# Attention slots with fixed PSUM bank roles, flip copies on two engines, and logarithms in the hybrid mask

## The chip, the cores and the metric

The kernel runs on one core of one Trainium2 chip. The metric is the device time of one execution in microseconds (us), lower is better. Engines are called by the profile's names: PE (TensorE, the matrix engine), DVE (VectorE), ACT (ScalarE), POOL (GpSimd) and SP (SyncE, which here only issues DMAs).

## The reference

A sequence of 256 positions and width 1024 passes through four layers in float32. Layer one (kind `a`): sliding-window attention with sinks, 16 heads, 2 key/value heads. Layer two (`b`): block attention, which for 256 positions is plain causal attention, 16 heads, 4 key/value heads. Layers three and four (`h`, the hybrids): 8 heads of attention beside a state space scan, and then a gated feed-forward part. Each attention is softmax(scores + mask) times values. In the hybrids three dilated windows are merged by their denominators:

```python
def dilated_attention(q, k, v):
    outs, lses = [], []
    for window, dilation in DILATED_PATTERNS:
        o, l = dilated_window_branch(q, k, v, window, dilation)
        outs.append(o)
        lses.append(l)
    wts = jax.nn.softmax(jnp.stack(lses, axis=0), axis=0)
    return jnp.einsum('ibshg,ibshgc->bshgc', wts, jnp.stack(outs, axis=0))
```

This equals one softmax in which each key counts as often as there are windows that hold it (0 to 3 times): a multiplicity per pair of positions.

## The kernel before, in words

The kernel is raw code for five engines, whose order is one list of steps, `sc.steps`, written out by `build_schedule` through `mixer_ab` (layers one and two) and `hybrid` (three and four). Every engine walks the same list and does its part of each step, so a step that stands earlier in the list is earlier on every engine; engines wait for each other by semaphores.

The bulk is projections. A step `chunk` is 12 matmuls for the first 128 positions, and the step `rest` behind it 12 for the second 128; a weight block of 512 columns takes two chunks (`halves`, one per half of the contraction). Weights are split into a high and a low part for precision: SP loads `raw` (L956), ACT rounds to `hi` (L1161), DVE or POOL forms `lo` (L901), two chunks ahead (`due`, `AHEAD`), and PE multiplies (L1000). The split of a chunk's step stands on each engine before the work put between `chunk` and `rest`.

Between `chunk` and `rest`, and between chunks, the lists of `halves`, `project_chunk` and `out_product` place other work (`goes_on`). One such piece is `attention(sc, n)`, slot n of a layer. It works on pairs of heads:

- `scores`: PE computes scores of two heads (L1052, L1055, 64-row tiles), each in its own bank of 128x384 f32 (three 128x128 blocks: the causal half of 256x256). DVE adds the mask and takes row minima of the negated scaled scores in place (L1644), ACT takes exponentials into `prob` (L1293, L1294).
- `flip`: PE transposes the three blocks of `prob` into a bank (L975). In layers one and two ACT copies the bank to `probT` (L1301); in the hybrids DVE does so and multiplies by the multiplicities `mult` (L1654).
- `pv`: PE multiplies `probT` by the values with a column of ones (L1075 to L1077), both heads into one bank, and ACT copies it out as `oev` (L1308).

Slot n of the kernel before does, in this order: outputs (`pv`, `oev`) of pair n-2, flips of pair n-1, scores of pair n. Layers one and two have slots 0 to 9, the hybrids 0 to 5.

PSUM has eight banks. Four (0 to 3) hold projections. The other four ("scratch banks", `NSCR`) are handed out by `Schedule.bank` in rotation to all small steps: flips, scores, outputs, and helpers such as `turn_q` and `turn_k` (transposes of queries and keys, copied by ACT at L1283 and L1277), `turn` (transposes of gated outputs or inputs: ACT copies at L1211, DVE subtracts at L1580, and only then is the bank free), `conv` (transposes at L975, ACT scales at L1333, DVE adds the other taps in six instructions at L1736 and frees the bank), `sums`, `decay` and others. PE waits in `freed` (L869) until the engine that last used the bank is done with it. A full slot takes five banks of four: the second bank of the scores is the one that the same slot's outputs used.

Where the slots stand: in `mixer_ab` slots 1, 2, 3 around the chunks of the first gate projection, with two `turn_q` steps ahead of slot 3; slot 4 right behind the two silus `ev_z` (L1244, with an ACT table load); slots 5 to 7 around the second gate projection, with `fill_gates` (on POOL, L1431 and L1436) behind slot 5; two `turn` steps ahead of slot 8; slot 9 inside the first chunk of the output product, and `fill_gates` of the second half behind that chunk's `rest`. In `hybrid`: slot 1 then `sums`; `conv` for block 0; slot 2 then `conv`; `conv_silu` (four silus on ACT, L1340, with a table load) then slot 3; `conv`; slot 4 then `conv`; `conv_silu` then slot 5 and `fill_gates`.

At the start ACT issues small loads (L1169 to L1177): sinks, positions, small rows, the masks (`mask_stage`, L1174), then the convolution taps (`taps_stage`, L1175 and L1177), which PE transposes once (L1020) ahead of the third projection.

Of the kernel before, what the change touches and what calls it, by code (L numbers as in the profile page):

```python
# [24 lines left out]
BF16 = mybir.dt.bfloat16  # L25
# [9 lines left out]
NEG = -1e30  # L35
# [26 lines left out]
C_SEL = C_MASK + 3 * QC + P  # L62
C_ALL = C_SEL + 32
M_SCAN, M_SEL = 3 * QC, 3 * QC + P


def constants():
# [7 lines left out]
    mult = [(d >= 0) * ((d <= 128).astype(np.float32) + (d % 4 == 0) + (d % 16 == 0)) for d in delta]  # L75
    for i, x in enumerate(mult):
        c[:, C_CT + i * P:C_CT + (i + 1) * P] = x.T
    inv = np.float32(10000.0) ** (-np.arange(0, HD, 2, dtype=np.float32) / np.float32(HD))
    for m in range(M):
# [8 lines left out]
        [x > 0 for x in mult],  # L88
# [5 lines left out]
    c[:, C_MASK + 3 * QC:C_SEL] = np.where(t > u, NEG, 0.0)  # L94
# [42 lines left out]
class Schedule:  # L137


    def __init__(self):  # L140
        self.steps, self.count, self.blocks, self.banks = [], {}, [], []
# [3 lines left out]
        self.heads, self.loaded, self.mult_flips, self.plain_flips = 0, 0, 0, 0  # L145
# [7 lines left out]
    def bank(self):  # L153
        n = len(self.banks)
        b = Bank(n % NSCR, self.banks[n - NSCR] if n >= NSCR else None)
        assert b.before is None or b.before.freed is not None, "a bank is taken before it is freed"
        self.banks.append(b)
        return b
# [56 lines left out]
def attention(sc, n):  # L215
# [182 lines left out]
def new_attention(sc, which, heads, nkv):  # L398
    if sc.heads:
        count_flips(sc)  # L400
# [4 lines left out]


def count_flips(sc):
    if sc.att["kind"] == "h":
        sc.mult_flips += len(sc.att["flip"])
    else:  # L410
        sc.plain_flips += len(sc.att["flip"])


def mixer_ab(sc, which, w_in, w_out, nkv, mid=False):
# [36 lines left out]
    if mid:  # L451
# [7 lines left out]
        0: (att(9), [lambda: fill_gates(sc, a, 1, zb)]),  # L459
# [3 lines left out]
def hybrid(sc, layer, w, last_gain):  # L463
# [108 lines left out]
    b = halves(sc, w_in, [(z0, 512)], do(conv_silu, 1) + att(5) + do(fill_gates, sc, a, 0, None), do(conv, 2, 0) + do(bback),  # L572
# [120 lines left out]
def build(nc, t):  # L693
# [37 lines left out]
    masks = keep("masks", [P, 3 * QC + P + 32], BF16)  # L731
# [21 lines left out]
    mult = cst[:, C_CT:C_CT + QC]  # L753
# [219 lines left out]
    def _(pe):  # L973
# [4 lines left out]
        for s in sc.steps:  # L978
# [87 lines left out]
            elif s.kind == "pv":  # L1066
# [3 lines left out]
                pe.wait_ge(sem["flip", "vector" if a["kind"] == "h" else "scalar"], a["flip"][hd].n + 1)  # L1070
# [80 lines left out]
    def _(act):  # L1151
# [37 lines left out]
        for s in sc.steps:  # L1189
# [106 lines left out]
            elif s.kind == "flip" and s.att["kind"] != "h":  # L1296
# [4 lines left out]
                done(nc.scalar.activation(A[f"probT{s.p % 2}"][:, :], psum[4 + s.bank.at][:, 0:QC], ACT.Copy), s)  # L1301
# [155 lines left out]
    def _(dve):  # L1457
# [81 lines left out]
        for s in sc.steps:  # L1539
# [99 lines left out]
            elif s.kind == "scores":  # L1639
                a, hd = s.att, s.head  # L1640
                dve.wait_ge(sem["scores", "tensor"], s.i + 1)
                bank, at_ = psum[4 + s.bank.at], {"a": 0, "b": 1, "h": 2}[a["kind"]] * QC
                for m, c in enumerate((slice(0, P), slice(P, QC))):
                    last = nc.vector.tensor_tensor_reduce(  # L1644
                        bank[:, c], bank[:, c], masks[:, at_ + c.start:at_ + c.stop], -SCALE,
# [3 lines left out]
            elif s.kind == "flip" and s.att["kind"] == "h":  # L1649
# [4 lines left out]
                done(tt(Hb[f"probT{s.p % 2}"][:, :], psum[4 + s.bank.at][:, 0:QC], mult, ALU.mult), s)  # L1654
# [160 lines left out]
```

## Time and profile before

| what | us |
|---|---|
| median of 3 runs | 920.56 |
| lowest and highest of the runs | 919.92, 925.25 |
| the profiled execution | 923.07 |
| its span (first to last instruction) | 921.2 |
| PE busy in the span | 882.9 |
| DVE, ACT, POOL busy | 558.5, 518.6, 127.7 |

The profiled execution's own time is its span and 1.9 us around it; it lies 2.5 us above the median. PE's busy time counts a matmul from its start to its modelled end, so neighbours overlap, and a row's length is a little more than the distance to the next start.

### The profile page before, as it was taken

Reading aid. Unit: us, or ns where it says so; the run is one execution under the profiler, and the core shown is the slowest. Engines: PE = TensorE matmul, PEld = TensorE weight load, DVE = VectorE, ACT = ScalarE, POOL = GpSimd, SP = SyncE. Lnnn points to the kernel's source line nnn. Section 1 sums busy time; section 2 is a strip of 40 time slices with the busy share of each in tenths; the row PEclk is TensorE's granted clock in tenths of the full one; section 3 lists DMA queues with packets and bytes.
Section 4 is the critical chain, followed back from the end, with each engine's and each line's share of the span. In section 5 each row is a group of like instructions: output and inputs, shape, how many; then the busy total and the mean of one; then the engine's idle time right before and its main releaser. Section 6 shows DMA issues by size and latency. Waiting matters only on the chain.

```text
span 921.2 us, 12293 instructions
## 1 busy us (share of the span) xinstructions
PE 882.9 (96%) x4557; PEld 728.8 (79%) x4557; DVE 558.5 (61%) x969; ACT 518.6 (56%) x853; POOL 127.7 (14%) x103
## 2 busy tenths in 40 slices
PE   4899998999999999999999999999999999999995
PEld 3787887878787888788888888887888888888884
DVE  4754578546766567865555544756677755555443
ACT  3567755676487685464444433677874644444331
POOL 0031103421015350000000000042430000000000
PEclk9899999999999999999999999999999999999998
DMA  8641344443544424576565555534423766565521
GB/s 279 218 150 57 129 163 157 140 129 102 177 167 139 137 93 136 164 236 187 188 185 183 183 183 185 193 104 139 137 92 120 246 190 188 186 190 189 196 95 46
DMA packets 94846, 146.88 MB, mean 159 GB/s; under 512 B 6476, under 2 KB 54852, under 8 KB 94788
## 3 DMA queue, kind: packets, MB, share of 16 engines
q1 hardware_dynamic: 91392, 139.14, 46.3%
q0 software_dynamic: 1440, 5.24, 2.0%
q10 hardware_dynamic: 1956, 1.71, 0.5%
q8 instruction: 37, 0.61, 0.3%
q14 instruction: 21, 0.17, 0.1%
HBM read 145.04 MB, written 1.05 MB: 159 GB/s over the span
## 4 chain that ended last, share of the span: by engine, by line
PE 70%; issue 21%; DVE 3%; ACT 2%; DMA 2%; POOL 0%; ACTq 0%; POOLq 0%; DVEq 0%
PE bank L1000 55%; PE bank L975 6%; PE bank L1141 1%; PE bank L1052 1%; PE bank L1055 1%; PE bank L1077 1%; PE bank L1076 1%; DMA taps_stage<-in_conv_b 1%; PE bank L1075 1%; DMA gains<-in_norm_g 1%; ACT junk L1186 1%; DVE lo L901 1%; ACT hi L1161 1%; DVE hyb_MT L1749 1%; PE bank L1120 0%
## 5 line engine op out<-in xcount | busy, mean ns | idle before, releaser
L901 DVE TENSOR_TENSOR lo<-raw,hi 128x1024 fp32r<-128x1024 f32 x246 | 302.4, 1254 | 133.7 <-ACT hi L1161 131.6
L1161 ACT ACTIVATE hi<-raw 128x1024 fp32r<-128x1024 f32 x262 | 268.4, 1056 | 77.0 <-PE bank L1000 69.9
L1000 PE MATMUL bank<-hi,xT_hi 128*128 128x512 f32 (+2 forms) x736 | 294.4, 400 | 8.5 <-DVE lo L901 3.1
L1000 PE MATMUL bank<-hi,xT_lo 128*128 128x512 f32 (+2 forms) x736 | 285.5, 388 | 0.0
L1000 PE MATMUL bank<-lo,xT_hi 128*128 128x512 f32 (+2 forms) x736 | 284.5, 387 | 0.0
L1000 PEld LDWEIGHTS bank<-hi,xT_hi 128*128 128x128 f32 x736 | 140.0, 190 | 41.6 <-issue 13.8
L1000 PEld LDWEIGHTS bank<-hi,xT_lo 128*128 128x128 f32 x736 | 139.6, 190 | 28.9
L1000 PEld LDWEIGHTS bank<-lo,xT_hi 128*128 128x128 f32 x736 | 140.3, 191 | 25.5 <-issue 0.5
L1000 PE MATMUL bank<-hi,hT 128*128 128x512 f32 x352 | 111.2, 395 | 0.0
L1000 PEld LDWEIGHTS bank<-hi,hT 128*128 128x128 f32 x352 | 66.3, 188 | 15.4
L1000 PE MATMUL bank<-lo,hT 128*128 128x512 f32 x176 | 69.4, 395 | 0.0
L1000 PE MATMUL bank<-hi,oT_hi 128*128 128x512 f32 x160 | 66.9, 418 | 0.0
L1000 PE MATMUL bank<-hi,oT_lo 128*128 128x512 f32 x160 | 62.7, 392 | 0.0
L1000 PE MATMUL bank<-lo,oT_hi 128*128 128x512 f32 x160 | 62.4, 390 | 0.0
L1208 ACT ACTIVATE hT<-bank 128x512 fp32r<-128x512 f32 x22 | 13.2, 598 | 77.2 <-PE bank L975 77.2
L1577 DVE TENSOR_TENSOR hT<-bank,hT 128x512 fp32r<-128x512 f32 x22 | 15.2, 692 | 59.3 <-ACT hT L1208 59.3
L975 PE MATMUL bank<-cst,quarter 128*128 128x128 f32 x264 | 39.4, 277 | 12.0 <-DVE quarter L1571 10.1
L1258 ACT ACTIVATE silu_gate<-bank,rms 128x256 f32<-128x256 f32 x44 | 20.7, 475 | 50.3 <-PE bank L1000 50.3
L975 PEld LDWEIGHTS bank<-cst,quarter 128*128 128x128 f32 x264 | 32.8, 143 | 20.2 <-issue 10.3
L901 POOL TENSOR_TENSOR lo<-raw,hi 128x1024 fp32r<-128x1024 f32 x16 | 38.2, 2399 | 74.1 <-ACT hi L1161 74.1
L1612 DVE SCALAR_TENSOR_TENSOR quarter<-bank,rms,silu_gate 128x256 f32<-128x256 f32 x44 | 19.3, 479 | 41.1 <-ACT silu_gate L1258 41.1
L1736 DVE SCALAR_TENSOR_TENSOR hyb_acc<-bank,taps,hyb_acc 128x255 f32<-128x255 f32 (+2 forms) x72 | 29.2, 474 | 19.9 <-ACT hyb_acc L1333 19.9
(230 smaller groups left out, 983.5 us busy)
## 6 DMA issues: line engine op xcount, KB each, us to landing
raw<-in_w_in SPq DMA_DIRECT2D x26, 1024.0 KB, 5.1
raw<-in_w_gate SPq DMA_DIRECT2D x44, 512.0 KB, 4.0
raw<-in_w_up SPq DMA_DIRECT2D x44, 512.0 KB, 4.9
raw<-in_w_down SPq DMA_DIRECT2D x22, 1024.0 KB, 4.9
raw<-in_w_out SPq DMA_DIRECT2D x20, 1024.0 KB, 5.1
raw<-in_w_in_b SPq DMA_DIRECT2D x10, 1024.0 KB, 5.1
raw<-in_w_in_a SPq DMA_DIRECT2D x8, 1024.0 KB, 7.8
gains<-in_norm_g POOLq DMA_DIRECT2D x2, 512.0 KB, 6.8
```

Source lines behind the costliest of these rows:

```text
L901: return engine.tensor_tensor(lo[r][:, cols], raw[c.i % RAW][:, cols], hi[r][:, cols].bitcast(F32), ALU.subtract)
L975: return nc.tensor.transpose(out, in_, ident)
L1000: last = nc.tensor.matmul(bank[:, 0:wd], still[a], mv[r][:, off:off + wd], start=c.first and i == 0 and j == 0, stop=c.last and i == len(t ...
L1052: nc.tensor.matmul(bank[:, 0:P], q[r:r + 64, hd // 2, 0:P], k[r:r + 64, kv, 0:P], start=True, stop=True)
L1055: nc.tensor.matmul(bank[:, P:QC], q[r:r + 64, hd // 2, P:S], k[r:r + 64, kv, 0:S], start=True, stop=True).then_inc(sem["scores", "tensor"], 1)
L1075: nc.tensor.matmul(bank[:, c0:c0 + W1], pt[:, 0:P], v[:, 0, kv, :], start=True, stop=True)
L1161: nc.scalar.activation(hi[c.i % SPLIT][:, cols], raw[c.i % RAW][:, cols], ACT.Copy)\
L1208: done(nc.scalar.activation(out, bank[:, :], ACT.Copy), s)
L1258: last = nc.scalar.activation(sil[s.i % 2][:, m, :], bank[:, 0:UPW], ACT.Silu, scale=rms[:, 1, m:m + 1])
L1577: done(tt(b, bank[:, :], a.bitcast(F32), ALU.subtract), s)
L1612: last = stt(quarter[s.buf][:, m * UPW:(m + 1) * UPW], psum[2 * s.block["pair"] + m][:, UPW:2 * UPW], rms[:, 1, m:m + 1], sil[s.i % 2][:, ...
L1736: ins = stt(acc[:, tap:S], x[:, 0:S - tap], cw[:, 3 - tap, ct:ct + 1], acc[:, tap:S], ALU.mult, ALU.add)
```

## The change

1. In `attention`, slot n does flips of pair n-1, scores of pair n, outputs of pair n-1. The last slot (9, or 5 in the hybrids) disappears from the lists, and `fill_gates` of the second half in `mixer_ab` moves from behind the `rest` of the output product's first chunk to between that `chunk` and its `rest`.
2. Banks have roles: scores of the even and odd head in banks 0 and 1, their flips in 2 and 3, outputs in bank 2. Other steps take the bank least recently taken, where scores count as taken three places later than they were.
3. The flip copy of the even head is on ACT, of the odd head on DVE, in all layers, as plain copies.
4. The hybrids' multiplicities m are added as log(m)/SCALE with the mask before the exponential, in f32 from `cst`, in place of the bf16 mask and the later multiplication. The mask tensor loses 384 of its 1312 columns.

```diff
-C_SEL = C_MASK + 3 * QC + P
+C_SEL = C_MASK + 2 * QC + P
@@ constants
-        c[:, C_CT + i * P:C_CT + (i + 1) * P] = x.T
+        c[:, C_CT + i * P:C_CT + (i + 1) * P] = np.where(x > 0, np.log(np.maximum(x, 1)) / SCALE, NEG)
@@ Schedule
-    def bank(self):
-        n = len(self.banks)
-        b = Bank(n % NSCR, self.banks[n - NSCR] if n >= NSCR else None)
+    def bank(self, at=None, later=0):
+        if at is None:
+            at = min(range(NSCR), key=lambda i: self.taken[i])
+        b = Bank(at, self.banks[at])
         assert b.before is None or b.before.freed is not None, "a bank is taken before it is freed"
-        self.banks.append(b)
+        self.banks[at] = b
+        self.clock += 1
+        self.taken[at] = self.clock + later
         return b
@@ attention
-    if 2 <= n <= pairs + 1:
-        a["obank"] = sc.bank()
-        for head in (2 * n - 4, 2 * n - 3):
-            s = sc.step("pv", head=head, att=a, bank=a["obank"], p=a["base"] + head)
-            a["pv"].append(s)
-        o = sc.step("oev", att=a, pair=head // 2, bank=a["obank"], pv=s)
-        a["obank"].freed = (o, "scalar")
-        a["oev"].append(o)
     if 1 <= n <= pairs:
         for head in (2 * n - 2, 2 * n - 1):
-            b = sc.bank()
-            s = sc.step("flip", head=head, att=a, bank=b, p=a["base"] + head,
-                        n=len(a["flip"]) + (sc.mult_flips if a["kind"] == "h" else sc.plain_flips))
-            b.freed = (s, "vector" if a["kind"] == "h" else "scalar")
+            b = sc.bank(2 + head % 2)
+            s = sc.step("flip", head=head, att=a, bank=b, p=a["base"] + head, n=(a["base"] + head) // 2)
+            b.freed = (s, "vector" if head % 2 else "scalar")
             a["flip"].append(s)
     if n < pairs:
-        b0, b1 = sc.bank(), sc.bank()
+        b0, b1 = sc.bank(0, 3), sc.bank(1, 3)
...
+    if 1 <= n <= pairs:
+        a["obank"] = sc.bank(2)
+        for head in (2 * n - 2, 2 * n - 1):
+            s = sc.step("pv", head=head, att=a, bank=a["obank"], p=a["base"] + head)
+            a["pv"].append(s)
+        o = sc.step("oev", att=a, pair=head // 2, bank=a["obank"], pv=s)
+        a["obank"].freed = (o, "scalar")
+        a["oev"].append(o)
@@ mixer_ab, out_product
-        0: (att(9), [lambda: fill_gates(sc, a, 1, zb)]),
+        0: ([lambda: fill_gates(sc, a, 1, zb)], ()),
@@ hybrid
-    b = halves(sc, w_in, [(z0, 512)], do(conv_silu, 1) + att(5) + do(fill_gates, sc, a, 0, None), do(conv, 2, 0) + do(bback),
+    b = halves(sc, w_in, [(z0, 512)], do(conv_silu, 1) + do(fill_gates, sc, a, 0, None), do(conv, 2, 0) + do(bback),
@@ ACT
-            elif s.kind == "flip" and s.att["kind"] != "h":
+            elif s.kind == "flip" and s.head % 2 == 0:
...
-                done(nc.scalar.activation(A[f"probT{s.p % 2}"][:, :], psum[4 + s.bank.at][:, 0:QC], ACT.Copy), s)
+                done(nc.scalar.activation(B[f"probT{s.p % 2}"][:, :], psum[4 + s.bank.at][:, 0:QC], ACT.Copy), s)
@@ DVE
+                mask = {"a": masks[:, 0:QC], "b": masks[:, QC:2 * QC], "h": log_mult}[a["kind"]]
...
-            elif s.kind == "flip" and s.att["kind"] == "h":
+            elif s.kind == "flip" and s.head % 2:
...
-                done(tt(Hb[f"probT{s.p % 2}"][:, :], psum[4 + s.bank.at][:, 0:QC], mult, ALU.mult), s)
+                done(nc.vector.tensor_copy(B[f"probT{s.p % 2}"][:, :], psum[4 + s.bank.at][:, 0:QC]), s)
```

## Rows read from the trace of the kernel before

**Rows 1.** The page, busy us, share of the span and instructions of PE first.
```profile
PE 882.9 (96%) x4557; PEld 728.8 (79%) x4557; DVE 558.5 (61%) x969; ACT 518.6 (56%) x853; POOL 127.7 (14%) x103
```

**Rows 2.** Waits of PE, whole span: total us, times, longest us.
```profile
PE bank L1020 <- DMA taps_stage<-in_conv_b: 3.1, 1, 3.1
...
PE bank L1052 <- ACT hyb_o L1308: 2.7, 2, 1.4
...
PE bank L1052 <- ACT attn_o L1308: 2.5, 2, 1.3
...
PE bank L975 <- DVE quarter L1683: 0.3, 1, 0.3
```

**Rows 3.** Timeline (start us, length us), PE and ACT, layer one slot 2.
```profile
62.00 0.33 PE L1075 MATMUL bank<-attn_v,attn_probT 128*128 128x65 f32 x2
...
63.28 0.82 PE L975 MATMUL bank<-cst,attn_prob 128*128 128x128 f32 x6
...
64.03 0.49 PE L1052 MATMUL bank<-attn_kT,attn_qT 64*128 64x128 f32 x4
...
64.89 0.50 PE L1000 MATMUL bank<-hi,xT_hi 128*128 128x512 f32 x1
...
67.15 1.06 ACT L1161 ACTIVATE hi<-raw 128x1024 fp32r<-128x1024 f32 x1
```

**Rows 4.** Timeline, PE and DVE, layer one slot 1.
```profile
57.49 0.81 PE L975 MATMUL bank<-cst,attn_prob 128*128 128x128 f32 x6
...
57.98 1.85 DVE L901 TENSOR_TENSOR lo<-raw,hi 128x1024 fp32r<-128x1024 f32 x1 [1.75 <-ACT hi L1161]
```

**Rows 5.** Lines L1301 and L1654: duration ns min/median/max.
```profile
L1301 ACT ACTIVATE attn_probT<-bank x32: 484/491/511, 58.0 to 215.5; 128x384 f32<-128x384 f32 x32
...
L1654 DVE TENSOR_TENSOR hyb_probT<-bank,cst x16: 547/550/558, 276.7 to 642.0; 128x384 f32<-128x384 f32 x16
```

**Rows 6.** Timeline, PE and ACT, query turns ahead of layer one slot 3.
```profile
67.75 1.03 PE L975 MATMUL bank<-cst,attn_q 128*128 128x128 f32 x8
...
68.39 1.08 ACT L1283 ACTIVATE attn_qT<-bank 128x512 f32<-128x512 f32 x2 [0.18 <-PE bank L975]
```

**Rows 7.** Timeline, ACT and PE, layer one slot 4.
```profile
74.85 1.28 ACT L1244 ACT_TABLE_LOAD   x1
...
76.15 1.26 ACT L1244 ACTIVATE attn_z<-bank,rms 128x512 f32<-128x512 f32 x2
...
77.84 0.49 PE L1052 MATMUL bank<-attn_kT,attn_qT 64*128 64x128 f32 x4 [1.30 <-ACT attn_o L1308]
```

**Rows 8.** Timeline, ACT and DVE, gate turns ahead of layer one slot 8.
```profile
99.49 1.09 ACT L1211 ACTIVATE oT_hi<-bank 128x512 fp32r<-128x512 f32 x2 [0.18 <-PE bank L975]
...
100.48 1.28 DVE L1580 TENSOR_TENSOR oT_lo<-bank,oT_hi 128x512 fp32r<-128x512 f32 x2
```

**Rows 9.** Timeline, layer three, slots 1, 2 and 4.
```profile
276.21 0.82 PE L975 MATMUL bank<-cst,hyb_prob 128*128 128x128 f32 x6
...
277.25 1.07 ACT L1161 ACTIVATE hi<-raw 128x1024 fp32r<-128x1024 f32 x1
...
284.05 2.43 DVE L1736 SCALAR_TENSOR_TENSOR hyb_acc<-bank,taps,hyb_acc 128x255 f32<-128x255 f32 x6 [2.07 <-ACT hyb_acc L1333]
...
284.51 0.33 PE L1075 MATMUL bank<-hyb_v,hyb_probT 128*128 128x65 f32 x2
...
286.73 0.49 PE L1052 MATMUL bank<-hyb_kT,hyb_qT 64*128 64x128 f32 x4
...
304.60 1.22 DVE L901 TENSOR_TENSOR lo<-raw,hi 128x1024 fp32r<-128x1024 f32 x1
```

**Rows 10.** DMA landings; windows of PE, PEld, DVE, ACT, POOL busy, PEclk, DMA, GB/s.
```profile
mask_stage<-in_cst ACTq DMA_DIRECT2D x1, 656.0 KB, 9.2
...
38.00:40.00 2.00, 1.45 (x4) 1.26 (x5) 1.97 (x3) 0.27 (x1) 0.00 (x0) 0.50 0.94 351
...
50.00:110.00 60.00, 58.70 (x370) 48.33 (x370) 30.70 (x85) 44.19 (x85) 14.70 (x13) 1.00 0.30 100
```

More of the change, by code:

```diff
@@ L61 @@
 C_MASK = C_KEEP
-C_SEL = C_MASK + 3 * QC + P
+C_SEL = C_MASK + 2 * QC + P
 C_ALL = C_SEL + 32
-M_SCAN, M_SEL = 3 * QC, 3 * QC + P
+M_SCAN, M_SEL = 2 * QC, 2 * QC + P
 def constants():
@@ L74, in constants @@
     c[:, C_U:C_U + P] = t <= u
-    mult = [(d >= 0) * ((d <= 128).astype(np.float32) + (d % 4 == 0) + (d % 16 == 0)) for d in delta]
+    mult = [(d >= 0) * ((d <= 128).astype(np.float64) + (d % 4 == 0) + (d % 16 == 0)) for d in delta]
     for i, x in enumerate(mult):
-        c[:, C_CT + i * P:C_CT + (i + 1) * P] = x.T
+        c[:, C_CT + i * P:C_CT + (i + 1) * P] = np.where(x > 0, np.log(np.maximum(x, 1)) / SCALE, NEG)
     inv = np.float32(10000.0) ** (-np.arange(0, HD, 2, dtype=np.float32) / np.float32(HD))
@@ L87, in constants @@
         [d >= 0 for d in delta],
-        [x > 0 for x in mult],
     )
@@ L93, in constants @@
             c[:, at:at + P] = np.where(x, 0.0, NEG)
-    c[:, C_MASK + 3 * QC:C_SEL] = np.where(t > u, NEG, 0.0)
+    c[:, C_MASK + 2 * QC:C_SEL] = np.where(t > u, NEG, 0.0)
     for part in range(3):
@@ L140, in __init__ @@
     def __init__(self):
-        self.steps, self.count, self.blocks, self.banks = [], {}, [], []
+        self.steps, self.count, self.blocks = [], {}, []
+        self.banks, self.taken, self.clock = [None] * NSCR, [0] * NSCR, 0
         self.parts, self.quarters, self.gains = 0, [], []
@@ L144, in __init__ @@
         self.pool_splits = []
-        self.heads, self.loaded, self.mult_flips, self.plain_flips = 0, 0, 0, 0
+        self.heads, self.loaded = 0, 0
     def step(self, kind, **of):
@@ L398, in new_attention @@
 def new_attention(sc, which, heads, nkv):
-    if sc.heads:
-        count_flips(sc)
     a = sc.att = {"kind": which, "heads": heads, "nkv": nkv, "scores": [], "flip": [], "pv": [], "oev": [],
@@ L404, in new_attention @@
     return a
[L407 to L411, printed above, removed]
 def mixer_ab(sc, which, w_in, w_out, nkv, mid=False):
@@ L730, in build @@
     cst = keep("cst", [P, C_KEEP])
-    masks = keep("masks", [P, 3 * QC + P + 32], BF16)
+    masks = keep("masks", [P, 2 * QC + P + 32], BF16)
     csum = keep("csum", [P, P], BF16)
@@ L752, in build @@
     ident, upper = cst[:, C_ID:C_ID + P], cst[:, C_U:C_U + P]
-    mult = cst[:, C_CT:C_CT + QC]
+    log_mult = cst[:, C_CT:C_CT + QC]
     base = place[0]
@@ L1069, in _ @@
                 kv = hd // (a["heads"] // a["nkv"])
-                pe.wait_ge(sem["flip", "vector" if a["kind"] == "h" else "scalar"], a["flip"][hd].n + 1)
+                pe.wait_ge(sem["flip", "vector" if hd % 2 else "scalar"], a["flip"][hd].n + 1)
                 bank = freed(pe, s.bank) if hd % 2 == 0 else psum[4 + s.bank.at]
@@ L1295, in _ @@
                                           bias=shift[:, hd, 1:2]), s)
-            elif s.kind == "flip" and s.att["kind"] != "h":
+            elif s.kind == "flip" and s.head % 2 == 0:
+                B = Hb if s.att["kind"] == "h" else A
                 act.wait_ge(sem["flip", "tensor"], s.i + 1)
@@ L1641, in _ @@
                 dve.wait_ge(sem["scores", "tensor"], s.i + 1)
-                bank, at_ = psum[4 + s.bank.at], {"a": 0, "b": 1, "h": 2}[a["kind"]] * QC
+                bank = psum[4 + s.bank.at]
+                mask = {"a": masks[:, 0:QC], "b": masks[:, QC:2 * QC], "h": log_mult}[a["kind"]]
                 for m, c in enumerate((slice(0, P), slice(P, QC))):
                     last = nc.vector.tensor_tensor_reduce(
-                        bank[:, c], bank[:, c], masks[:, at_ + c.start:at_ + c.stop], -SCALE,
+                        bank[:, c], bank[:, c], mask[:, c], -SCALE,
                         sinks[:, 1, hd:hd + 1] if a["kind"] == "a" else BIG, ALU.add, ALU.min,
@@ L1648, in _ @@
                 done(last, s)
-            elif s.kind == "flip" and s.att["kind"] == "h":
+            elif s.kind == "flip" and s.head % 2:
+                B = Hb if s.att["kind"] == "h" else A
                 dve.wait_ge(sem["flip", "tensor"], s.i + 1)
```

## The prediction, made before the changed kernel was built or run

> **What bounds the kernel now.** I read the page's first part, then TensorE's waits, then the timeline of single attention slots on TensorE, ScalarE (ACT) and VectorE (DVE). TensorE is busy for 882.9 of 921.2 us [rows 1], so only two things can change the time: work that TensorE itself does, and gaps in its stream. The change keeps every TensorE instruction (six transposes, four scores matmuls and six output matmuls a pair of heads), so only gaps count. TensorE's waits name few of them [rows 2]: four slots wait for the copy of the outputs (2.7 + 2.5 = 5.2 us), one gate quarter costs 0.3, the taps 3.1. The rest lies at the start and in the norms, which the change leaves alone.
>
> A whole slot runs from 62.00 (outputs) over 63.28 (flips) and 64.03 (scores) to 64.89, the next weight matmul [rows 3]: 2.89 us, of which outputs 1.28, flips 0.65 to 0.75, scores the rest. Then come 12 weight matmuls (2.87, to 67.75 in rows 6) and the next slot. ACT has finished the exponentials 2.26 us after the scores' end and only then splits weights (67.15) [rows 3]; DVE's split follows, 1.22 us when alone [rows 9]. A producer's end reaches the waiting engine after about 0.2 us from TensorE and 0.15 from ACT or DVE: four of the eight transposes from 67.75 are through at 68.19 (0.109 each, as 0.65 for six), and ACT starts at 68.39 [rows 6].
>
> **The change part by part.** Four edits move TensorE's gaps.
>
> *1. Scores get banks of their own.* Now the second scores bank is the outputs' bank of the same slot, so scores wait for ACT's output copy. The 1.30 us at 77.84 [rows 7], its three siblings, a hidden 0.2 in slot 2 of layer three (scores at 286.73, 2.22 after 284.51 [rows 9], where rows 3 have 2.03) and the gate's 0.3 go: -5.7.
>
> *2. Outputs move into the slot of their flips.* Order in a slot: flips, scores, outputs. From slot start T: flips end T+0.65, scores T+1.55, first outputs may start T+1.55, second T+2.17. The even head's copy on ACT costs 0.49 [rows 5] and is ready at 0.33+0.2+0.49+0.15 = T+1.2. The odd head's on DVE isn't in the trace: from above the 0.55 of the multiply that it replaces, from below half of that, since it reads one operand for two [rows 5]; I take 0.5, near the multiply, which reads the same bank into the same tile. At 0.28 the terms below lose 0.2 each in six places, 1.3 in all. It is ready at T+1.55. So a slot with both engines idle gets no wait. The exceptions, each an engine busy at T:
> - Slot 1 of the first two layers: DVE, slowed beside GpSimd's rotation, splits until 57.98+1.85 = 59.83 against T = 57.49 [rows 4]; copy and signal end at 60.4, wanted at 59.66: 0.75 each, 1.5 together.
> - Slot 1 of layer three: ACT's split ends at 278.32, where T = 276.21 [rows 9]; copy to 278.9, wanted 277.76: 1.15. In layer four ACT is free: 0.
> - Slot 4 (layers one and two) and slot 3 (three and four): ACT loads a table and does the silus, 1.28 + 1.26 [rows 7] (four silus in the hybrids). Exponentials now end 1.3 earlier against the next slot, but the output copy (0.4) comes before the split; the load starts at T-0.4 and the even copy is ready at T+2.8, wanted T+1.55: 1.25, 1.25, 1.3, 1.3 = 5.1. The old wait is thus replaced, not removed.
> - Slot 6 of layers one and two, where GpSimd's gates stretch DVE's split to about 1.9: 0.25 each, 0.5.
> - Slot 8 of layers one and two has no scores between flips and outputs: the even copy is wanted at T+0.65, ready T+1.12: 0.47 each, 0.9.
> - Slot 4 of the hybrids: DVE's split of 304.60, 1.22 long [rows 9], stands ahead of the odd copy; outputs come 0.7 late, twice: 1.4.
>
> *3. Flips are tied to banks 2 and 3, and other work takes the banks least recently taken.* I followed the taking of banks. Scores' banks are marked three places younger, so a helper before a slot gets 3 and then 2, and the slot's first flip needs 2 at once. Before, the outputs' 1.28 us and the rotation covered that.
> - Query turns before slot 3 of layers one and two: eight transposes from 67.75 end at 68.62 (0.87); ACT's copies end at 68.39+1.08 = 69.47 [rows 6]; with the signal 69.62: 1.0 each, 2.0.
> - Gate turns before slot 8: ACT starts at 99.49, so by the spacing of rows 6 the transposes ran from 98.85 to 99.72; ACT's pair ends at 100.58 and DVE's second subtraction (1.28 for two) about 0.7 later [rows 8]; with the signal 1.73 late each, 3.5. I let DVE's own split no longer be what it queues behind; if it still is, 2.2 each.
> - The first convolution before slot 2 of the hybrids: its bank is 2, and DVE's six taps end at 284.05+2.43 = 286.48 while the slot starts at 284.51 [rows 9], 2.1 late. The sums ahead of it move back with the slot and lose a queue of 0.4: 1.7. The same chain in layer four, whose rows repeat these, ends 1.1 late instead of 2.0: 1.0 after the change. Together 2.7.
> - The second convolution before slot 4 holds bank 3: the odd flip waits 0.57, twice: 1.1.
>
> *4. Masks shrink by 384 columns.* Their load is 656 KB and lands 9.2 us after issue [rows 10]; the taps, issued behind it, are what TensorE waits 3.1 for [rows 2]. 192 KB less is 0.56 us at the 351 GB/s of that time [rows 10], and 2.7 at the mask's own pace (656 KB in 9.2 us), of which much is waiting to start; I take 0.9. More would be worth more: behind this gap the granted clock is 0.50 [rows 10], the lower of the two levels (1.2 of 2.4 GHz), about 2.6 us for 13 matmuls. I expect that it stays. The DVE cast of masks gets shorter behind other work, and f32 logarithms in place of a bf16 mask lie in a pass beside weight matmuls: 0, between -0.1 and +0.5 over the 16 heads.
>
> **Sum.** New waits: 1.5 + 1.15 + 5.1 + 0.5 + 0.9 + 1.4 (edit 2, 10.6) and 2.0 + 3.5 + 2.7 + 1.1 (edit 3, 9.3) = 19.9. Gone: 5.7 and 0.9. Net +13.3. Against the profiled execution (923.07 us, span 921.2) that is 936.4; against the median of 920.56, 933.9. The dropped last slot of each layer saves nothing, since its outputs are done one slot earlier.
>
> Two rules of the Trainium skill speak here. The trace has the table load at 1.28 and the silu right behind it, at 76.15 after 74.85 [rows 7]. "ScalarE: Activation LUTs", What ACT_TABLE_LOAD costs, adds a drain of about 1.38 us to each switch; four slots would then lose 5.5 more. The trace shows no such drain, so I leave it out.
>
> **The rivals.**
> - *The copies hide (12%).* If helpers have left bank 2 and both copies fit under the scores everywhere, only the removals stay: 920.56 - 6.6 = 914.0. For it: ordinary slots have 0.6 us of room (wanted T+2.17, ready T+1.55). Against it: rows 6, 8 and 9 show the holders still working after T. It decides if the waits before flips and outputs sum to less than 6.6 us.
> - *Only banks and tables bind (22%).* DVE's and ACT's splits drift earlier, as exponentials now end earlier, and the remaining copy waits (5.5) vanish: 933.9 - 5.5 = 928.4.
> - *The clock falls as well (16%).* After the 3.1 us gap the granted clock was 0.50; the 1.30 us gap at 77.84 [rows 7] left it at 1.00 over 50 to 110 us [rows 10]. The new 1.7 + 0.5 in slot 8 lies between. A fall costs some 2.6 us of matmuls; in both slots, 939.1. "TensorE: Matmul & The Clock Gate", A second HAM failure mode, says that small idles from cycling PSUM banks can make the clock oscillate; if that held in all eight stalled slots, the time would be near 955, which the clock of 1.00 around the present stalls of 1.2 to 1.4 us doesn't bear out.
>
> The forecast has 50%, 929 to 939 of its own.
>
> **How the numbers follow.** About 1% is what a measurement of this kernel tells from no change: 911.4 and 929.8 are the bounds. Slower: 0.44 of the forecast, 0.05 of the second rival, 0.15 of the third: 0.64. Faster by over 1% would need the first rival and the taps gap with its slow clock gone as well: 0.04. The rest, 0.32, is within. Range 922 to 941: it cuts off the first rival and the far end of the third.
>
> **What would show it.** Right: TensorE waits for ACT at the query flips (1.0) and for DVE at the gate flips (1.7) and at the flips after the first convolution (1.0 to 1.7); output matmuls wait for DVE's copy in slot 1 and behind table loads by 1.2 to 1.3; scores never wait for the outputs; the taps gap is 2 to 2.6. Wrong: no TensorE wait on flips, or named new waits under 10 us in sum; a taps gap under 1 us with the clock at 1.00 behind it; or a granted clock under 0.9 inside the attention stretches.

## The result and the profile after

The changed kernel takes 937.62 us (median of four runs, 931.89 to 938.57) where the kernel before takes 920.79 beside it (919.92 to 925.25): a ratio of 1.0157, 95% interval 1.0112 to 1.0202. It is slower. A second comparison of the same kernel, told below, gives 1.0137 (1.0112 to 1.0161) and a median of 931.81.

The profiled execution after took 931.89 us with a span of 930.0; the one before had 923.07 and 921.2. First the page's first part, for [rows 1]:

```profile
span 930.0 us, 12293 instructions
...
PE 883.9 (95%) x4557; PEld 727.6 (78%) x4557; DVE 559.3 (60%) x977; ACT 515.4 (55%) x845; POOL 125.5 (13%) x103
```

PE has the same 4557 matmuls and is busy for 1.0 us more than in [rows 1], so what came is almost all gaps. On balance eight copies moved from ACT to DVE (845 against 853, 977 against 969): sixteen of the first two layers went to DVE and eight of the hybrids to ACT. The waits of PE over the whole span (total us, times, longest), for [rows 2]:

```profile
PE bank L968 <- DVE oT_lo L1574: 3.3, 2, 1.7
...
PE bank L1068 <- ACT hyb_probT L1295: 2.9, 3, 1.0
...
PE bank L1013 <- DMA taps_stage<-in_conv_b: 2.7, 1, 2.7
...
PE bank L968 <- DVE hyb_acc L1732: 2.4, 4, 0.8
PE bank L1068 <- ACT attn_probT L1295: 2.2, 4, 0.8
PE bank L968 <- ACT attn_qT L1276: 1.7, 2, 0.8
...
PE bank L1068 <- DVE hyb_probT L1650: 0.7, 2, 0.4
PE bank L1068 <- DVE attn_probT L1650: 0.7, 2, 0.4
```

The four waits for output copies (5.2 us in [rows 2]) are gone, and no scores matmul waits at all. In their place stand three rows of waits of flips for their bank (L968: oT_lo, hyb_acc, attn_qT, 7.4 us together) and four rows of waits of output matmuls for a flip copy (L1068, 6.5 us): 13.9 us of named waits. (Lines have moved: transposes L975 to L968, scores L1052 to L1045, outputs L1075 to L1068, ACT's flip copy L1301 to L1295, DVE's L1654 to L1650.)

Single slots show each kind. The timeline (start, length, engine and line, what it waited for) of layer one, slots 1, 3, 4 and 8:

```profile
56.76 1.84 DVE L894 TENSOR_TENSOR lo<-raw,hi 128x1024 fp32r<-128x1024 f32 x1 [1.75 <-ACT hi L1154]
...
58.52 0.55 DVE L1650 COPY attn_probT<-bank 128x384 f32<-128x384 f32 x1
...
59.12 0.44 PE L1068 MATMUL bank<-attn_v,attn_probT 128*128 128x65 f32 x2 [0.37 <-DVE attn_probT L1650]
...
69.11 1.08 ACT L1276 ACTIVATE attn_qT<-bank 128x512 f32<-128x512 f32 x2 [1.25 <-PE bank L968]
70.34 0.84 PE L968 MATMUL bank<-cst,attn_prob 128*128 128x128 f32 x6 [0.83 <-ACT attn_qT L1276]
...
75.58 1.28 ACT L1237 ACT_TABLE_LOAD   x1
...
76.19 0.81 PE L968 MATMUL bank<-cst,attn_prob 128*128 128x128 f32 x6
76.88 1.26 ACT L1237 ACTIVATE attn_z<-bank,rms 128x512 f32<-128x512 f32 x2
...
78.03 0.49 ACT L1295 ACTIVATE attn_probT<-bank 128x384 f32<-128x384 f32 x1
...
78.67 0.41 PE L1068 MATMUL bank<-attn_v,attn_probT 128*128 128x65 f32 x2 [0.81 <-ACT attn_probT L1295]
...
101.53 1.29 DVE L1574 TENSOR_TENSOR oT_lo<-bank,oT_hi 128x512 fp32r<-128x512 f32 x2 [0.61 <-ACT oT_hi L1204]
102.96 0.85 PE L968 MATMUL bank<-cst,attn_prob 128*128 128x128 f32 x6 [1.66 <-DVE oT_lo L1574]
...
104.15 0.41 PE L1068 MATMUL bank<-attn_v,attn_probT 128*128 128x65 f32 x2 [0.34 <-ACT attn_probT L1295]
```

Read each as a chain. Slot 1: the split of 56.76 ends at 58.60, DVE's copy follows it and ends at 59.07, and the odd head's outputs start then. Slot 3: ACT's copy of the query turns ends at 70.19 and the flips start 0.15 later. Slot 4: the flips are there at 76.9, but ACT is in the table load and the silus until 78.1, and the even head's outputs wait 0.81. Slot 8: DVE's second subtraction ends at 102.82, and only then is bank 2 free for the first flip. Layer three: outputs of slot 1, flips of slot 2 behind the first convolution, and slot 4 with both waits:

```profile
283.78 0.41 PE L1068 MATMUL bank<-hyb_v,hyb_probT 128*128 128x65 f32 x2 [0.95 <-ACT hyb_probT L1295]
...
290.14 2.43 DVE L1732 SCALAR_TENSOR_TENSOR hyb_acc<-bank,taps,hyb_acc 128x255 f32<-128x255 f32 x6 [2.15 <-ACT hyb_acc L1327]
...
292.72 0.85 PE L968 MATMUL bank<-cst,hyb_prob 128*128 128x128 f32 x6 [0.80 <-DVE hyb_acc L1732]
...
312.59 0.52 PE L968 MATMUL bank<-cst,hyb_prob 128*128 128x128 f32 x3 [0.41 <-DVE hyb_acc L1732]
...
314.10 0.44 PE L1068 MATMUL bank<-hyb_v,hyb_probT 128*128 128x65 f32 x2 [0.37 <-DVE hyb_probT L1650]
```

A wait row counts from the modelled end of the last matmul, and in a running stream the next matmul starts before that end: the eight gate turns start at 100.27 and are through 8 x 0.109 later, at 101.14, where their row ends at 101.30. So a stop costs some 0.2 us more than its row says, and the slots must be measured as well. The measure used from here on is the slot distance: from the start of the last weight matmul before a slot to the start of the first one behind it. Over all slots and the gate quarters it grows by 18.3 us where it grows. It falls by 5.6 where the old waits were, and by 0.6 because the last slots are gone: +12.1 (the table further down has the parts).

Executions of the changed kernel scatter more than those of the kernel before (standard deviation 3.2 us over 14 against 1.5 over 45), and they differ with TensorE's mean granted clock: over the 14, 929.31, 930.33 and 930.37 at a mean of 0.998; 931.16 to 932.38 at 0.996; 935.08 to 935.34 at 0.989 to 0.991; 936.88 to 938.57 at 0.986 to 0.989. A straight line through all 14 has 0.66 us for each 0.001 of the mean. The kernel before has 0.991 to 0.997; the line through its 41 executions with a recorded clock has 0.81. At equal clock the two lines differ by about 13 us: 931.5 against 918.2 at 0.996, 934.8 against 922.2 at 0.991.

The two profiled executions differ by only 8.8 us of span. The slots account for +12.1 and the taps gap for -0.4 (2.7 for 3.1). The rest, about -3, is the clock: the execution before had 0.69 at 152 to 156 us and 0.68 and 0.50 at 36 to 44, the one after 1.00, and 0.78 and 0.79.

### The profile page after: what moved, and what is told of

It is laid out like the page before. It is cut to its first block, busy times and chain, and to the rows that moved or that the text cites. A ratio compares the mean times of both kernels' runs of the same rounds, so it can differ in the third digit from the quotient of the medians.

```text
span 930.0 us, 12293 instructions
## 1 busy us (share of the span) xinstructions
PE 883.9 (95%) x4557; PEld 727.6 (78%) x4557; DVE 559.3 (60%) x977; ACT 515.4 (55%) x845; POOL 125.5 (13%) x103
## 4 chain that ended last, share of the span: by engine, by line
PE 62%; issue 22%; DVE 8%; ACT 5%; DMA 2%; POOL 0%; ACTq 0%; POOLq 0%; DVEq 0%
PE bank L993 49%; PE bank L968 5%; DVE lo L894 2%; PE bank L1068 1%; PE bank L1134 1%; ACT hi L1154 1%; PE bank L1070 1%; PE bank L1069 1%; DMA taps_stage<-in_conv_b 1%; DVE hyb_acc L1732 1%; ACT junk L1179 1%; DMA gains<-in_norm_g 1%; PE bank L1048 1%; PE bank L1045 1%; DVE hyb_MT L1745 1%
## 5 line engine op out<-in xcount | busy, mean ns | idle before, releaser
L968 PE MATMUL bank<-cst,quarter 128*128 128x128 f32 x264 | 39.8, 279 | 11.9 <-DVE quarter L1565 10.2
L968 PEld LDWEIGHTS bank<-cst,quarter 128*128 128x128 f32 x264 | 33.0, 144 | 20.2 <-issue 10.4
```

The source lines that it names most:

```text
L968: return nc.tensor.transpose(out, in_, ident)
```

## The experiments

The theory to test was the prediction's: the change costs in two ways, flips that wait for a helper's bank, and outputs that wait for copies. Rivals: the order of the slots itself, the logarithms and the plain copy, or the clock. All kernels but two are the changed kernel, as it is or with a part undone; `log_only` and `outputs_dve` start from the kernel before. Each is compared with the others in two ways: by its time against the lines above at the same mean clock, and by the slot distances of its trace.

**1. The changed kernel again,** with no edit, timed beside the next three.

> The changed kernel itself, profiled and timed once more. Its profiled execution took 931.9 us at a mean clock of 0.996, its other executions 935 to 939 us at 0.986 to 0.991. Theory 1 (new waits of TensorE are the loss, the clock is a separate lottery that both kernels take part in): a median near 937 us against 921; where the clock is lower, it is low behind the long gaps that the kernel before has too (the taps near 38 us, the issue gap near 150 us), not in attention slots. Theory 2 (the new stalls pull the clock down): windows at half clock behind slot 8 of the first two layers or in the hybrids' slots.

Measured: 931.81 (929.31 to 936.88, six runs) against 920.64 (17 runs of the kernel before); ratio 1.0137 (1.0112 to 1.0161). The slowdown repeats. The median is lower because four of these six executions had a mean clock of 0.996 or more; the two at 0.986 and 0.989 took 936.88 and 935.34. The median near 937 that theory 1 expected was the lower clock's. Its waits of flips and outputs are those of the first profile.

**2. `lru_banks`: the roles of the banks undone.** Every piece takes the bank least recently taken; order, copies and logarithms stay.

```diff
-            b = sc.bank(2 + head % 2)
+            b = sc.bank()
...
-        b0, b1 = sc.bank(0, 3), sc.bank(1, 3)
+        b0, b1 = sc.bank(), sc.bank()
...
-        a["obank"] = sc.bank(2)
+        a["obank"] = sc.bank(a["flip"][2 * n - 2].bank.at)
```

> Only the bank roles undone: every step takes the least recently taken bank, the outputs take the bank of the even flip. Theory 1: flips no longer wait for query turns (1.7 us in the changed kernel's profile), gate turns (3.3) and convolutions (2.4), so 7.4 us less than the changed kernel, about 930 us, and at most 0.5 us of waits on other banks in their place. Rival (the order is what costs, the flips' waits only hide waits of the outputs for their copies): the output matmuls then wait 2 us or more longer in the same slots and the time stays above 934 us.

Measured: 926.72 (924.36 to 928.43, six runs); ratio 1.0062 (1.0044 to 1.008). PE's waits:

```profile
PE bank L1068 <- ACT hyb_probT L1295: 3.6, 5, 1.0
...
PE bank L1068 <- ACT attn_probT L1295: 2.5, 4, 0.8
...
PE bank L1045 <- ACT attn_qT L1276: 0.3, 2, 0.2
```

No flip waits for a helper. Copy waits stay and grow a little (7.6 for 6.5, with 0.8 and 0.7 on DVE's copies), since slots that start on time ask for their copies earlier. In slot 4 of the hybrids this takes back the whole gain, as the rival had it: the flip's wait of 0.41 is gone, the even output waits 0.34 in its place, and the slot distance stays at 3.72. In all the slot distances fall by 6.0, and against the changed kernel's line at the same clock (0.9938, 933.0) the run saves 6.6: half the slowdown is the bank roles. The expected 930 was reckoned from executions at a lower clock, so the 926.7 is not a larger gain than the 7.4 foretold but a smaller one.

**3. `later_zero`: the roles stay, the offset of three goes.** Helpers then take scores' banks as well as the flips'.

```diff
-        b0, b1 = sc.bank(0, 3), sc.bank(1, 3)
+        b0, b1 = sc.bank(0), sc.bank(1)
```

> Only the mark that makes the scores' banks three places younger is taken away; roles and order stay. A pair of helpers before a slot then gets banks 3 and 0 in place of 3 and 2. Theory 1 (the second helper sits in the even flip's bank): the flips' wait for query turns falls from 0.83 us each to under 0.2, that for gate turns from 1.66 to about 0.85 (the odd flip still waits for the first turn), the first convolutions' from 0.8 to about 0.5 (now a wait of the scores); 3.5 us less than the changed kernel at the same clock, 928 to 929 us. Rival (the wait is for the helper's copy whichever bank it sits in): no more than 1 us less.

Measured: 928.83 (928.45 to 929.26, four runs at 0.991 to 0.993), ratio 1.0096 (1.008 to 1.0112). Its waits on banks:

```profile
PE bank L968 <- DVE oT_lo L1574: 1.5, 2, 0.7
...
PE bank L968 <- DVE hyb_acc L1732: 0.8, 2, 0.4
...
PE bank L1045 <- DVE hyb_acc L1732: 0.4, 2, 0.3
```

The flips' waits fall from 7.4 to 2.3, and scores gain 0.4. The slot distances fall by 5.2 of the 6.0 that undoing the roles gives, and at the same clock the time falls by 5.6 of 6.6 (3.5 was expected): most of what the roles cost comes from the one argument that marks scores' banks as younger, so that helpers land on the banks that the next slot's flips need. In slot 8 the wait moves from the first flip (1.66) to the odd one (0.74), and the output wait behind it goes.

**4. `table_slots_dve`: in the four slots behind a table load, DVE copies both flips.** (Semaphores are counted by engine for that.)

```diff
-            s = sc.step("flip", head=head, att=a, bank=b, p=a["base"] + head, n=(a["base"] + head) // 2)
-            b.freed = (s, "vector" if head % 2 else "scalar")
+            who = "vector" if head % 2 or n == (3 if a["kind"] == "h" else 4) else "scalar"
+            s = sc.step("flip", head=head, att=a, bank=b, p=a["base"] + head, n=sc.flips[who], what=who)
...
+            b.freed = (s, who)
```

> The changed kernel with both flip copies on DVE in the four slots where ACT stands behind a table load and silus. Theory 1: the waits of output matmuls for ACT's copy in these slots (0.81, 0.69, 0.98, 0.97 us) shrink to 0.3 or less each, so 3 us less than the changed kernel, about 934.5 us. Rival (ACT's lateness only moves on, to the exponentials and the weight split behind them): the next slots get waits for ACT and the gain is under 1 us.

Measured: 931.03 (930.23 to 931.62, four runs, all at 0.990 to 0.992, where the changed kernel's line has about 935); ratio 1.0112 (1.0095 to 1.0129). Layer one, slot 4:

```profile
77.51 1.02 DVE L1653 COPY attn_probT<-bank 128x384 f32<-128x384 f32 x2
...
78.56 0.44 PE L1071 MATMUL bank<-attn_v,attn_probT 128*128 128x65 f32 x2
```

The outputs no longer wait, and the waits for ACT's copies fall from 2.9 + 2.2 to 0.9 + 0.7. The four slots shorten to 3.19 and 3.20, the distance of an ordinary slot, by 3.6 us together; at equal clock the time falls by 4.2. The table slots are worth 3.6 to 4.2 us, not 5.1. The next slots get no wait for ACT, so the rival is out.

**5. `lru_and_table_dve`: both of these,** to see what is left.

> The rotation of banks (run lru_banks) together with both flip copies on DVE in the four slots behind table loads (run table_slots_dve). Theory 1: the two gains add, -5.1 to -6.7 and -3.6 at the same clock, so 922.5 to 923.5 us, still 2 us above the kernel before, because slot 1's and slot 8's waits (some 2.4 us) stay and the old order has none of them. Rival (they overlap, one behind the other in the same slots): 925 us or more.

Measured: 922.09 (917.64 to 924.74, twelve runs), ratio 1.0021 (1.0006 to 1.0037). The two gains add, as theory 1 had it: the slot distances fall by 9.6, which is 6.0 and 3.6, and at equal clock the time falls by 10.4 where the two runs alone gave 6.6 and 4.2. Left over the kernel before are 2.5 of the 12.1 us by slot distances and 2.8 at equal clock. These are the copy waits of slots 1 and 8 and of the hybrids' slot 4, and the ordinary slots (below), less the old waits; no run removes them one by one.

**6. `old_order`: the slots' old order and rotation,** with the two-engine copies and the logarithms kept.

```diff
+    if 2 <= n <= pairs + 1:
+        a["obank"] = sc.bank()
+        for head in (2 * n - 4, 2 * n - 3):
...
-            b = sc.bank(2 + head % 2)
+            b = sc.bank()
...
-        b0, b1 = sc.bank(0, 3), sc.bank(1, 3)
+        b0, b1 = sc.bank(), sc.bank()
...
```

The outputs behind the scores go, and the last slots come back to the lists.

> The order of the slots and the rotation of the banks as before the change; the copies on two engines and the logarithms in the mask stay. Theory 1: the four waits of scores for the output copy are back (5.2 us), none of the 13.9 us of new waits is left, the taps gap is 2.7 in place of 3.1: 920.5 us, the same as before the change within 1.5 us. Rival (odd copies behind DVE's splits cost in this order too): 924 us or more, with output matmuls or flips waiting for DVE.

Measured: 922.64 (917.56 to 924.37, twelve runs), ratio 1.0017 (1.0003 to 1.0032), most of them at 0.991 or 0.992, where the kernel before has about 922: 0.7 us slower at equal clock. By medians it is 2.0 above, a little outside the expected 1.5. Its waits are those of [rows 2] again, and one more, in slot 1 of layer three, where the matmuls of `sums` wait for the bank that ACT's flip copy holds:

```profile
PE bank L1045 <- ACT hyb_o L1302: 2.7, 2, 1.4
...
PE bank L1045 <- ACT attn_o L1302: 2.5, 2, 1.3
...
PE bank L1076 <- ACT hyb_probT L1295: 0.9, 1, 0.9
```

That slot takes 3.46 us where the kernel before has 2.50, and slot 2 behind it 3.54 for 3.73; all other slot distances are those of the kernel before. So two engines for the copies cost 0.8 us, all of it in layer three, and no output matmul waits for DVE: the rival is out. The slowdown is the new order with its roles.

**7. `log_only`: logarithms alone in the kernel before,** with the smaller mask and DVE's plain copy.

```diff
-C_SEL = C_MASK + 3 * QC + P
+C_SEL = C_MASK + 2 * QC + P
...
-                done(tt(Hb[f"probT{s.p % 2}"][:, :], psum[4 + s.bank.at][:, 0:QC], mult, ALU.mult), s)
+                done(nc.vector.tensor_copy(Hb[f"probT{s.p % 2}"][:, :], psum[4 + s.bank.at][:, 0:QC]), s)
...
```

The table of logarithms and the mask argument change as in the change above.

> The kernel before with the logarithms in the mask alone: smaller mask load, f32 mask in the hybrids, a plain DVE copy in place of the multiplication, in the old order and rotation. Theory 1: worth nothing that can be measured, 920 to 921 us; the taps gap varies between 2.7 and 3.8 us from execution to execution, and a plain copy takes 0.56 us as the multiplication took 0.55. Rival (192 KB less ahead of the taps shorten the gap): the taps gap is under 2.5 us and the time 1 us or more below the kernel before.

Measured: 921.44 (917.24 to 923.66, twelve runs), ratio 1.0005 (0.9991 to 1.002). No difference can be told, and at equal clock it is 0.2 us. PE at the taps, and the mask's landing (KB, us from issue):

```profile
37.91 0.46 PE L1019 MATMUL bank<-cst,taps_stage 120*128 120x120 f32 x1 [2.59 <-DMA taps_stage<-in_conv_b]
...
mask_stage<-in_cst ACTq DMA_DIRECT2D x1, 464.0 KB, 8.4
```

The mask lands 0.8 earlier than in [rows 10]. The gap is 2.6 us here, but 3.1, 3.3 and 3.9 in `old_order`, `lru_banks` and `later_zero`, which have the same small mask, and 2.6 to 3.1 over five executions of the changed kernel: it varies by more from execution to execution than the edit moves it, and the time doesn't follow.

**8. `outputs_dve`: `log_only`, and DVE copies the outputs out in the four table slots.** This attacks the wait that the change was exposed to, without moving anything: ACT is busy behind its table load, and DVE takes the one copy.

```diff
-        o = sc.step("oev", att=a, pair=head // 2, bank=a["obank"], pv=s)
-        a["obank"].freed = (o, "scalar")
+        who = "vector" if n == (3 if a["kind"] == "h" else 4) else "scalar"
+        o = sc.step("oev", att=a, pair=head // 2, bank=a["obank"], pv=s, what=who, n=sc.oevs[who])
+        sc.oevs[who] += 1
+        a["obank"].freed = (o, who)
```

> The kernel before with the logarithms in the mask and one change more: in the four slots behind table loads DVE, not ACT, copies the outputs out, so that scores needn't wait behind ACT's silus. Theory 1: the four waits of scores (1.30, 1.18, 1.33, 1.37 us) shrink to 0.3 or less each, 4.5 us less than before: 916 us, faster than both kernels. Rival (another wait takes the place at once, for the exponentials or the weight split): 919 us or more.

Measured: 914.27 (911.53 to 916.25, six runs), ratio 0.9938 (0.992 to 0.9956): 5.7 us faster than the kernel before by medians (920.0, 23 runs) and 5.0 at equal clock, and faster than the changed one. Layer one, slot 4:

```profile
73.56 1.28 ACT L1253 ACT_TABLE_LOAD   x1
73.57 1.23 DVE L910 TENSOR_TENSOR lo<-raw,hi 128x1024 fp32r<-128x1024 f32 x1 [1.75 <-ACT hi L1170]
...
74.72 0.42 DVE L1663 COPY attn_o<-bank 128x260 f32<-128x260 f32 x1
...
75.29 0.49 PE L1061 MATMUL bank<-attn_kT,attn_qT 64*128 64x128 f32 x4
```

The copy (0.42 us) slips in between DVE's split and its next work, the scores start at 75.29 with no wait, PE's waits name no output copy any more, and the distance between the weight matmuls around the slot is 3.25 us for 4.50 before. The four slots together get 5.2 us shorter.

**9. `look_one`, `look_two`, `look_three`: three more profiled executions of the changed kernel,** for the clock.

> The changed kernel once more for its profile alone: where does the granted clock fall in a slower execution (935 us and more at a mean of 0.986 to 0.989)? Theory 1 (falls behind the taps gap and the issue gap only, which the kernel before has as well): low windows at 36 to 46 and 152 to 160 us alone, and a time on the line of about 0.6 us for each 0.001 of mean clock. Theory 2 (the new waits pull it down too, as at 104 to 108 us in the profile of table_slots_dve and at 280 to 288 us in that of later_zero): in some profile a low window inside an attention stretch.

> A second profile for the same question, with the same expectations: Theory 1 low windows at 36 to 46 and 152 to 160 us alone; theory 2 in some profile of the changed kernel a low window inside an attention stretch, costing some 2 us each.

> A third profile for the same question, with the same expectations as the two looks before: theory 1 low windows only behind the taps gap and the issue gap; theory 2 also one inside an attention stretch.

Measured: 935.08 (mean clock 0.989), 930.37 (0.998) and 931.16 (0.996), beside 918.8 for the kernel before. The first shows what the third rival foretold. Timeline of layer two's slot 8, and the windows of 4 us from it on (us, then PE, PEld, DVE, ACT, POOL busy with counts, granted clock, DMA share, GB/s):

```profile
218.85 0.85 PE L968 MATMUL bank<-cst,attn_prob 128*128 128x128 f32 x6 [1.66 <-DVE oT_lo L1574]
...
220.04 0.41 PE L1068 MATMUL bank<-attn_v,attn_probT 128*128 128x65 f32 x2 [0.34 <-ACT attn_probT L1295]
```
```profile
220.00:224.00 4.00, 3.96 (x16) 3.70 (x17) 0.29 (x1) 1.42 (x2) 0.00 (x0) 0.55 0.28 110
224.00:228.00 4.00, 4.00 (x12) 3.10 (x12) 1.40 (x3) 3.41 (x5) 0.00 (x0) 0.60 0.00 0
```

The profiled execution of the comparison above has the same waits at the same place and keeps its clock:

```profile
220.00:224.00 4.00, 3.86 (x23) 3.48 (x24) 0.39 (x1) 2.27 (x4) 0.00 (x0) 1.00 0.28 110
224.00:228.00 4.00, 4.00 (x20) 3.30 (x19) 2.22 (x4) 3.28 (x5) 0.82 (x1) 1.00 0.00 0
```

In the 8 us from 220, PE gets 28 matmuls at 0.55 and 0.60 and 43 at 1.00. From the last weight matmul before slot 8 to the next gate quarter `look_one` takes 16.7 us, and `look_two` 13.5: the fall cost 3.3 us. It is not the only one in `look_one`: the clock was also low from 152 to 159 us (0.52 and 0.63 in its two windows), where the kernel before and `log_only` fall too, and that stretch cost 2.9 us. So about half of what the clock cost in this execution lies where the kernel before falls as well.

`table_slots_dve` has a fall behind layer one's slot 8 (0.61 at 104 to 108 us). Counted over all traces with these two stops, the clock fell in 2 of 12 passes over slot 8; in the seven traces without stops of this length there, in none of 14. That the stops are the cause is read from the place and from these few cases. On average they cost little: the mean clock is 0.9926 over the changed kernel's 14 executions and 0.9934 over 41 of the kernel before, a difference of some 0.5 us.

## Why the prediction came out as it did

Right were the direction, the mechanism and the places. Each new wait of the prediction but slot 6's stands in the trace, and the sum of +13.3 us meets 13 at equal clock; both medians (937.62, 931.81) lie within the own range of 929 to 939, on either side of the 934.0. The median of the 14 executions is 933.7. The agreement of the sum is better than that of its terms, and part of it is luck: errors of both signs cancel. Measured here are the slot distances of both profiled traces, less that of an ordinary slot:

| term | predicted | measured |
|---|---|---|
| slot 1, layers one and two | 1.5 | 1.1 |
| slot 1, layers three and four | 1.15 | 1.0 |
| table slots | 5.1 | 3.6 |
| slot 6 | 0.5 | 0 |
| query turns before slot 3 | 2.0 | 2.0 |
| slot 8, banks and copies | 3.5 + 0.9 | 5.0 |
| first convolution | 2.7 | 1.9 |
| slot 4 of the hybrids, bank and copy | 1.1 + 1.4 | 2.2 |
| ordinary slots | 0 | 1.3 |
| removed by scores' own banks | -5.4 | -5.6 |
| gate quarter of layer one | -0.3 | +0.2 |
| last slots dropped | 0 | -0.6 |
| smaller mask | -0.9 | 0 |
| sum | +13.3 | +12.1 |

- *The copies.* DVE's plain copy takes 0.55 to 0.56 us, as the multiply did; I had taken 0.5, and the lower end of 0.28 is out. In slot 8 the even copy was put at T+1.12, though the same copy stood at T+1.2 a few lines earlier; the outputs start 1.19 after the flips. In slot 1 of the first layers the odd outputs start 2.85 after the slot's start (59.12 - 56.27) where I had 2.91, and an ordinary slot is itself 0.07 longer than I had: 0.57 each for 0.75. In slot 6 both fit under the scores.
- *Table slots, the largest error.* The step that failed is "the load starts at T-0.4 and the even copy is ready at T+2.8". It starts at T-0.61 (75.58 against 76.19), and the copy starts at T+1.84, a little ahead of the silus' recorded end; it ends at T+2.33 and the outputs start at T+2.48. Four times 0.3 to 0.5 too much. The mechanism holds: experiment 4 takes the copy off ACT and all four slots shrink to the ordinary distance, 3.6 us in all.
- *First convolution of layer three.* "The sums ahead of it move back with the slot and lose a queue of 0.4" was too little: 1.7 became 0.96. Before, the decay chain ran beside GpSimd's split, one cast of it took 1.09 us and ended 0.08 after the split did, and ACT got to the decays only 0.69 after the convolution's transposes (282.01 against 281.32), so that it scaled the convolution 1.87 after them:

```profile
280.09 1.09 DVE L1721 CAST csum<-hyb_rest 32x128 bf16<-32x128 f32 x1
...
281.32 0.60 PE L975 MATMUL bank<-cst,hyb_xin 128*128 128x128 f32 x4
...
282.01 0.22 ACT L1321 ACTIVATE hyb_dec<-hyb_dif 128x16 f32<-128x16 f32 x1 [1.96 <-DVE csum L1724]
...
283.19 0.82 ACT L1333 ACTIVATE hyb_acc<-bank,taps 128x256 f32<-128x256 f32 x2
```

  Above is the timeline of the kernel before, below that of the kernel after. There the chain starts after GpSimd's split has ended, the cast takes 0.22, the decays are done before the transposes start, and ACT scales 0.69 after them:

```profile
288.03 0.22 ACT L1315 ACTIVATE hyb_dec<-hyb_dif 128x16 f32<-128x16 f32 x1 [2.30 <-DVE csum L1720]
...
288.58 0.60 PE L968 MATMUL bank<-cst,hyb_xin 128*128 128x128 f32 x4
...
289.27 0.84 ACT L1327 ACTIVATE hyb_acc<-bank,taps 128x256 f32<-128x256 f32 x2
```

  The cast took 1.09 to 1.11 us in the three traces with the old order and both hybrid copies on DVE, 0.46 in `old_order`, and 0.22 in the nine others. The lag of 2.1 lost 1.18, not 0.4. Layer four, which had no such cast in my term (1.0), came out at 0.90.
- *Slot 8.* The flip waits 1.66 and the output 0.34, each with some 0.2 beyond its row: 2.48 a layer for my 2.2. My 1.73 and 0.47 were measured from the matmuls' issue, so they compare with 1.82 (101.14 to 102.96) and 0.54 (104.15 against 102.96 + 0.65); the rest is 0.07 as in every slot and about 0.05 that I can't place.
- *Ordinary slots.* Not in the sum at all: a slot takes 3.20 for 3.13, and 18 slots (2 to 7 of the first two layers, 2 to 4 of the hybrids) carry this 0.07. Outputs now follow scores directly, from 64-row tiles to 128-row ones, and that step costs about 0.07 more than the old one. This cause is argued from the place of the gap; no experiment isolates it.
- *The dropped last slots.* "Saves nothing" was wrong by a little: outputs in a slot of their own took 1.50 (1.49 in layer two), and slot 1 grew by 1.37 when they moved into it. With 0.16 in each hybrid that is 0.6 in all.
- *The gate quarter.* Its 0.30 was booked as gone with the scores' banks, but it waits for DVE's product `quarter` and not for a bank. It is 0.16 after the change, and the next gap there grew from 0.59 to 0.92.
- *The smaller mask.* "I take 0.9" failed. The load lands earlier (8.4 to 8.5 us for 9.2) and the gap varies from 2.6 to 3.9 between kernels that all have it; `log_only` measures 1.0005 for it and the logarithms together.
- *The clock.* "I expect that it stays" was too firm: the low stretch behind the taps is gone in `again`, `look_one` and `look_two`, with gaps of 2.7 to 3.1, and there in `look_three` with 2.6. The third rival is part of the truth: behind slot 8 the clock fell in one of the changed kernel's five profiled executions, for 3.3 us where the rival had 2.6. The spread from 930 to 938 us goes with the mean clock; which falls made up the slowest executions isn't known, as those had no trace.
- *The signs.* The waits at the query flips (0.83) and the gate flips (1.66) and the one for DVE's copy in slot 1 stand as foretold. Behind the first convolution it is 0.80 and 0.73 where 1.0 to 1.7 stood, behind table loads 0.69 to 0.98 where 1.2 to 1.3 stood; the taps gap of 2.7 lies just outside 2 to 2.6. One of the signs of being wrong, a granted clock under 0.9 inside the attention stretches, was met in `look_one` and in no other profile of the changed kernel.

The first rival (copies hide, 914.0) is out: named waits sum to 13.9. So is the second (928.4): of the 5.5 us of copy waits that were to vanish only slot 6's 0.5 went. The Trainium skill's drain behind a table load ("ScalarE: Activation LUTs", What ACT_TABLE_LOAD costs) is again absent: the load of 75.58 ends at 76.86 and the silu starts at 76.88, 0.02 later. Of what the Trainium skill says on bank cycling and the clock ("TensorE: Matmul & The Clock Gate", A second HAM failure mode) the runs bear out a weak form: one fall behind slot 8 in `look_one`, one in `table_slots_dve`, none behind the stops of 0.4 to 1.0 us in any trace of the changed kernel. `later_zero` has one behind a stop of 0.94 us in slot 1 of layer three (0.83 and 0.74 in the two windows from 280). The time near 955 that eight such falls would give is out.

## What to carry to other kernels

A buffer with a fixed role ties its next user to whoever was put there meanwhile, so the allocation of helpers matters more than that of the main steps: one argument (`later`) made up 5.2 of the 6.0 us of slot distances that the roles cost. Moving a consumer into the slot of its producer needs both copying engines idle at that moment; ask first which engine sits behind a table load or a split, and hand it the copy that is wanted last, as the 0.42 us copy on DVE did for 5 us at equal clock. And where executions of one kernel spread by 9 us with the mean granted clock, compare at equal clock before reading a difference of 5, and check that the change itself isn't what moves the clock.

## What the runs showed of the hardware

- The granted clock fell behind stops of 2.0 us in sum (slot 8, 1.66 and 0.34) in 2 of 12 passes, with the same rows each time, and once behind one of 0.94 (`later_zero`). Gaps of 2.7 and 3.1 at the taps left it at 1.00 in some executions. The length of the stop alone doesn't decide it. The fall in `look_one` lasted about 7 us and cost 3.3.
- 0.001 of mean clock was about 0.66 us of this kernel's time.
- A DVE cast of 32x128 that was under way while GpSimd's split ran took 1.09 us and ended 0.08 after the split; in traces where it came after the split it took 0.22. With it a whole chain moved. A cast out of PSUM beside the same split (96x128, 0.28) was not longer; which difference between the two matters isn't tested.
- A plain f32 copy from PSUM on DVE (128x384, 0.56 us) costs what a multiply by a second operand costs (0.55).
